# A transformer layer pair on one core: the expert selections move from GpSimd to VectorE, and the attention scores of two heads stand side by side

## The reference

```python
logit = einsum('hqd,hkd->hqk', q, k) * 64 ** -0.5 - slope[h] * (t_q - t_k)   # masked where t_k > t_q
p = softmax(logit)
out = einsum('hqk,hkd->hqd', p, v)
```

```python
sc = einsum("thpk,hpnk->thpn", q, sub_keys)                 # 512 tokens, 8 heads, 2 halves, 128 keys
s_top, i_top = lax.top_k(sc, 16)
cand = s_top[:, :, 0, :, None] + s_top[:, :, 1, None, :]
cand_idx = i_top[:, :, 0, :, None] * 128 + i_top[:, :, 1, None, :]
best, pos = lax.top_k(cand.reshape(n_tok, 8, 256), 16)
idx = take_along_axis(cand_idx.reshape(n_tok, 8, 256), pos, axis=-1)
g = softmax(best)
out = sum_k g * gelu(u_tab[idx] . x) * v_tab[idx]
```

## Time and profile before

| | |
|---|---|
| median of 3 runs | 2410.72 us (2405.76, 2410.72, 2411.18) |
| the profiled execution | 2405.64 us, span 2403.9 us |
| mean granted TensorE clock | 0.952 |
| PE busy | 2158.7 us, 90% of the span |
| DVE busy | 1690.5 us, 70% |
| ACT busy | 819.6 us, 34% |
| POOL busy | 771.1 us, 32% |

### The profile page before, as it was taken

One profiled execution on the slowest core, in us unless ns is written; L12 is line 12 of the kernel. 1 busy time (PEld: TensorE's weight loads), 2 busy tenths in 40 slices (PEclk: granted clock), 3 DMA queues, 4 the chain that ended last, 5 costly groups with the idle time before them and its releaser, 6 DMA issues. The chain is left out here.

```text
span 2403.9 us, 36262 instructions
## 1 busy us (share of the span) xinstructions
PE 2158.7 (90%) x11207; PEld 1887.0 (78%) x11207; DVE 1690.5 (70%) x3352; ACT 819.6 (34%) x1408; POOL 771.1 (32%) x677
## 2 busy tenths in 40 slices
PE   5998988475999997796979999999998999999997
PEld 4776677364777776686879999999997888888885
DVE  3675545536877763499478888788876888888886
ACT  4443322212222230423424444444432333333333
POOL 1000033000000000147546877887753222222220
PEclk9998999787999998898989999999998999999999
DMA  4431100013424222602256878878688999999995
GB/s 112 83 70 36 18 1 0 22 58 87 112 63 126 63 55 70 199 20 78 95 178 228 295 249 273 295 254 267 227 299 304 333 335 339 337 337 339 336 339 205
DMA packets 229948, 428.88 MB, mean 178 GB/s; under 512 B 18516, under 2 KB 155892, under 8 KB 229620
## 3 DMA queue, kind: packets, MB, share of 16 engines
q1 hardware_dynamic: 170976, 254.85, 34.1%
q0 software_dynamic: 41472, 151.01, 18.3%
q10 hardware_dynamic: 17428, 22.14, 2.6%
HBM read 381.80 MB, written 46.14 MB: 178 GB/s over the span
## 5 line engine op out<-in xcount | busy, mean ns | idle before, releaser
L1847 PE MATMUL bank<-xt_hi,u_hi 128*128 128x384 f32 x896 | 309.3, 345 | 0.0
L2127 PE MATMUL bank<-xt_hi 128*128 128x512 f32 x768 | 302.3, 394 | 7.6 <-DVE xt_lo L2056 7.6
L1847 PE MATMUL bank<-xt_hi,u_lo 128*128 128x384 f32 x896 | 300.6, 336 | 0.0
L1847 PE MATMUL bank<-xt_lo,u_hi 128*128 128x384 f32 x896 | 300.1, 335 | 0.0
L2127 PE MATMUL bank<-xt_hi,xt_lo 128*128 128x512 f32 x768 | 299.8, 390 | 0.0
L2127 PE MATMUL bank<-xt_lo,xt_hi 128*128 128x512 f32 x768 | 299.8, 390 | 0.0
L1709 POOL DMA_INDIRECT row_slot<-in_peer_v_dram,row_index x128 | 139.2, 1088 | 392.7 <-DVE row_x L2060 373.4
L2103 ACT ACTIVATE xt_hi<-xh 128x1024 fp32r<-128x1024 f32 x128 | 135.8, 1061 | 338.4 <-PE bank L2127 332.9
L1378 POOL TENSOR_TENSOR k_wlo<-k_raw,k_whi 128x2048 fp32r<-128x2048 f32 x4 | 18.4, 4604 | 615.8 <-ACT k_whi L1498 615.8
L2053 DVE TENSOR_TENSOR xt_lo<-xh,xt_hi 128x1024 fp32r<-128x1024 f32 x128 | 156.9, 1226 | 83.8 <-ACT xt_hi L2103 82.4
L1788 POOL TENSOR_TENSOR u_two<-u_match,u_weight_hi 128x512 fp32r<-128x512 f32 x96 | 179.7, 1872 | 96.8 <-DVE u_match L1874 96.3
(11 more groups left out here) (430 smaller groups left out, 4908.1 us busy)
## 6 DMA issues: line engine op xcount, KB each, us to landing
xh<-in_peer_v_dram SPq DMA_DIRECT2D x128, 512.0 KB, 5.4
xh<-in_peer_u_dram SPq DMA_DIRECT2D x113, 512.0 KB
x_raw<-in_w_in_dram SPq DMA_DIRECT2D x56, 512.0 KB, 7.0
v_ga<-acts SPq DMA_DIRECT2D x128, 192.0 KB, 5.4
acts<-xh ACTq DMA_DIRECT2D x112, 192.0 KB
weights<-u_spread POOLq DMA_DIRECT2D x32, 512.0 KB
v_gg<-weights SPq DMA_DIRECT2D x128, 128.0 KB
p_raw<-in_w_in_dram SPq DMA_DIRECT2D x12, 1024.0 KB
```

The costliest lines, as they stand in the source:

```text
L1847: mm = pe.matmul(k.ps[4 + b][:, 0:DENSE], w[b][:, c, :], x[:, c, 0:DENSE], start=(c == 0 and w is uhi and x is hi), stop=(c == DC - 1 and ...
L2127: mm = pe.matmul(k.ps[q][:, :], h[b][:, t * P:(t + 1) * P], v[b][:, f], start=False, stop=False, skip_group_check=True)
```

## The change

In the attention the steps are reordered to `p`, `qt`, `b`, so the two heads of a pair follow each other at the same width, and TensorE issues their scores together, in every second iteration. In the expert choice VectorE makes the selections of all four steps, each right behind its comparisons, and GpSimd's list is only the four low halves of the query weights and the sixteen early ones.

```diff
@@ attention
-        steps = [(p, b, qt) for p in range(2) for b in range(2) for qt in range(TT)]
+        steps = [(p, b, qt) for p in range(2) for qt in range(TT) for b in range(2)]
...
                     for n in range(n_steps):
-                        if n + 2 < n_steps:
+                        if n % 2 == 0 and n + 2 < n_steps:
                             score(i, n + 2)
+                            score(i, n + 3)
@@ choose_experts, GpSimd
-                order = Chain(pool, s["pool"], done=1)
-
-                def select(i, n):
-
-                    pool.wait_ge(s["matched"], after(2 * i + n + 1))
-                    order(pick(pool, i, n))
-                    for w in (8, 4, 2):
-                        order(pool.tensor_tensor(eq[n][:, :, :, 0:w], eq[n][:, :, :, 0:w], eq[n][:, :, :, w:2 * w], ALU.add))
-                    pool.tensor_tensor(sel[:, n, i, :, :], eq[n][:, :, :, 0], eq[n][:, :, :, 1], ALU.add
-                                       ).then_inc(s["reduced"], 1)
-                low(pool, 4)
-                low(pool, 5)
-                low(pool, 6)
-                select(0, 0)
-                select(0, 1)
-                low(pool, 7)
-                select(1, 0)
-                select(1, 1)
+                for sec in range(4, sections):
+                    low(pool, sec)
...
-                for e in range(5):
+                for e in range(EARLY):
                     low_early(e)
-                select(2, 0)
-                for e in range(5, EARLY - 1):
-                    low_early(e)
-                select(2, 1)
-                low_early(EARLY - 1)
@@ choose_experts, VectorE, at the end of each step i
+                    for n in range(2):
+                        dve.wait_ge(s["matched"], after(2 * i + 1 + n))
+                        order(pick(dve, i, n))
+                        dve.tensor_reduce(sel[:, n, i, :, :], eq[n][:, :, :, :], AX_X, ALU.add).then_inc(s["reduced"], 1)
-
-                for n in range(2):
-                    dve.wait_ge(s["matched"], after(2 * steps - 1 + n))
-                    order(pick(dve, steps - 1, n))
-                    dve.tensor_reduce(sel[:, n, steps - 1, :, :], eq[n][:, :, :, :], AX_X, ALU.add).then_inc(s["reduced"], 1)
```

More of the change, by code:

```diff
@@ L1364, in choose_experts @@
         names = ("residual_out", "keys_in", "keys_turned", "sc_kept", "read", "vec", "matched",
-                 "reduced", "shifted", "exped", "sel_done", "turned", "pool")
+                 "reduced", "shifted", "exped", "sel_done", "turned")
         s = {n: k.sem(f"k_{n}") for n in names}
```

## The result

The changed kernel takes 2384.67 us (median of 4 runs, 2381.74 to 2386.31), the one before, on the same chip, 2408.24 us (4 runs, 2404.75 to 2411.18). The ratio is 0.9901, with a 95% interval of 0.9882 to 0.9921: 23.6 us less, between 19 and 28. The profiled execution took 2385.49 us (span 2383.6), 20.2 less than that of before, at a mean granted clock of 0.954.

A forecast was written before the change was run, and what follows sets the result against it. TensorE was taken to bound the attention and VectorE the end of the expert choice. Terms of -11.7 us (-21.0 + 9.3) and -5 us (scores and idling), from 2410.7 us, gave 2394 us, range 2384 to 2405.

The forecast's parts named there:

- The scores, -5.9 us: Attention: two heads' scores side by side cost three of four record lengths, saving 5.9 us, between 0 and 11.8.
- The upper bound, -11.8 us: Attention: the second score of each pair is hidden wholly behind the first, saving 11.8 us.
- Rival (a): Attention: scores run wholly side by side, part 2 gives -12 us, time 2387 us; chance 0.13.
- a pair of 1.1 us: Attention: sign of a wrong forecast, a pair of 512-key scores taking 1.1 us where some 1.6 was expected.
- Idling behind ScalarE, +1 us: Attention: TensorE waits for ScalarE before the turn in 384-key steps, +1 us over eight quarters, within 0 to +4.
- -21.0 us for the wait, the excess and the comparisons, against the added selections: Expert choice, VectorE: -33.79 wait, -12.2 slow searches, -2.06 comparisons, +27.1 for three added selections, without any shutting out.
- The shutting out, +9.3 us: Expert choice: GpSimd's low halves hold up VectorE's instructions, 9.3 us over the four steps, between 0 and 39.
- The end of the stage: Expert choice: ends 9 to 15 us sooner, TensorE waiting near 20 us for the last copies, early tiles done by 1185.
- (b): Expert choice: VectorE is hardly shut out because GpSimd waits instead; -21 - 5, 2385 us; chance 0.13.
- (c): Attention: scores give nothing, running one after the other or turning into waits for ScalarE; -11.7 alone, 2399 us; chance 0.14.
- (d): Expert choice: some nine low halves hold VectorE up in full, 21.4 us; 2406 us, no change; chance 0.07.
- (e): Expert choice, steps 1 to 3: the lock in full size, 2.38 us per early low half, up to 2424 us; chance 0.04.

The follow-up runs named there:

- short_low_halves: The changed kernel with each early low half on GpSimd cut to 64 of its 1024 columns; expert choice 182.4 us instead of 193.9, time 2370.45 us (one run).
- attention_alone: The kernel before with only the attention's edit, selections left as before; 2392.49 us, 0.9946 of the kernel before.

## Why the prediction was right, and where it was not

Forecast 2394 us, measured 2384.67: the gain was 23.6 us and not 16.7, and 2.5 of the 9.3 us between the two times are the kernel before, whose median came out at 2408.24 and not at 2410.72. The time lies within the range of 2384 to 2405 by 0.7 us, and outside of the 2389 to 2398 that the forecast itself had. That it lies within at all is partly luck. By the stages the attention gave 13.2 us instead of 5, and the expert choice 8.0 instead of 11.7; had the second been as forecast, the time would have been about 2381.

- **The scores, -5.9 us: mis-sized.** The step that failed is that a second head's first record could only run beside the first head's second, so that three of four lengths were left. A pair takes one length. The upper bound, -11.8 us, is what the starts of matmuls show, and busy time says -14.0. Rival (a) is what happened in this part, and with it the rule of the Trainium skill that the prediction weighed (TensorE: Matmul & The Clock Gate, "Part 3: Packing small matmuls — row/col tiling"): the trace agrees, since two records for each score did not stand in the way. Taking the middle of two bounds was no reading of a row. The prediction itself named a pair of 1.1 us as a sign of being wrong, and a pair of 512 keys took 1.13.
- **The clock: a term that the prediction put at nothing.** The sum has no line for it. Time at the lower level fell from 21.6 to 14.7 us, by the estimate above up to 3.5 us of the 13.2.
- **Idling behind ScalarE, +1 us: was +2.4**, within its range of 0 to 4, and at the place named: 0.78 us in front of the turn at the steps with 384 keys, where 0.3 to 0.8 was said.
- **-21.0 us for the wait, the excess and the comparisons, against the added selections: right.** The window of waiting is gone, a step that nothing disturbs takes 44.3 us, and the last part 3.47.
- **The shutting out, +9.3 us: mis-sized, 13.1 us.** The mechanism was right (short_low_halves takes nearly all of it away). The split was 0.9, 2.5, 5 and 0.9 for the four steps; it was 1.1, 4.4, 7.6 and 0. The step that failed is the count of held instructions in step 1 and 2: in step 1 both products were held, 2.2 us each, and in step 2 two small instructions of the search, one of the two comparisons, one product in full and the other for 0.3 us. That a reduction costs nothing was right. Step 3 had none since only three low halves were left for its search, which, like that of before, was not held. The early low halves began 78.7 us behind the first search, and 78.6 were said.
- **The end of the stage: right in kind.** It ends 8.0 us sooner, where 9 to 15 were said. TensorE waited 28.0 us for the last copies where 20 were said, as its tiles were done even earlier. VectorE did not wait for the exponent; ScalarE waited 11.7 us for the shift in front of it, and the last early tile's activation stood behind that (at 1178.68) without anyone waiting for it.
- **The rivals.** (b), VectorE hardly shut out, is excluded by the 13.1 us: its time (2385) was met by other causes. (c) is excluded by attention_alone. (d) and (e) would need nine and more low halves that hold VectorE for their full length; 13.1 us is five and a half.

The total alone would have been no proof of the steps. Only the parts apart showed that the attention gave more than half of it, and only the time at each clock level that not all of that is the scores.

## What to carry to other kernels

Two matmuls with a contraction of 64, in different halves of the partitions and in different banks, belong side by side, and where they can't be, zeros up to 128 rows were cheaper here than a lone 64-row matmul between full ones (107.6 against 117.8 us of attention, and 104.6 side by side). Work goes to the engine that is idle at that time, stage by stage: taking all selections from GpSimd was worth 8 us, leaving it those of step 0, when it idles, another 11.5 us of the stage. Before giving VectorE instructions with two inputs, or casts and copies, ask how long GpSimd's instructions beside them are, for each one can be held for that length; cutting them in four took 5.4 us off the stage, though not off the time. When a stage of TensorE changes its length, hold the time at each clock level beside it before the whole is put down to the edit.

## What was new about the hardware

- A pair of float32 scores of two heads takes the time of one, although each is two records: 0.42 and 0.85 us to the next matmul at 128 and 384 keys, and 0.70 and 1.13 us long at 256 and 512, where a lone one had 0.42, 0.84, 0.70 and 1.12.
- A lone score of 64 rows between matmuls of 128 rows costs 0.33 us more than the same score padded with zeros, 0.1 in front and 0.23 behind; two neighbours in the same 64 rows pay about 0.2 us of the second part once.
- A waiting low half gets in at the next boundary between two back-to-back instructions of VectorE (2.28 us becomes 4.43 to 4.51), small ones with one input included (the copy of 8 elements took 1.31 us, the cast of 256 took 2.13). With GpSimd's instruction cut in four the same product took 2.82 us.
